# A mixer and mixture-of-experts kernel on one core: the first block's layers written in another order, its input norm done by rows, small loads moved to GpSimd

## What is computed

```python
def first_block(x, ...):
    h = _layernorm(x, ln_in_g, ln_in_b)
    for layer in range(DEPTH):                       # DEPTH = 2
        proj = jnp.einsum('bsd,de->bse', h, w_in[layer])   # 1024 x 4100
        (aq, ak, av, ag, bq, bk, bv, bf, bg, cq, ck, cv, cg) = jnp.split(proj, SPLIT_POINTS, axis=-1)
        # a: rotary, 4 heads, softmax(s1) - lam * softmax(s2), a norm per head
        # b: 4 heads, softmax with a running sum of log_sigmoid(bf) (forgetting)
        # c: 4 heads, stick breaking: exp(log_sigmoid(z) + later log_fail)
        y = concat([oa * silu(ag), ob * silu(bg), oc * silu(cg)]) @ w_out[layer]
        h = _layernorm(DEEPNORM_ALPHA * h + y, ln_g[layer], ln_b[layer])
    return h
```

## Time and profile before

| | us |
|---|---|
| median of 3 runs | 1777.88 (1777.81 to 1778.83) |
| the profiled execution, its own time | 1779.8 |
| its span, first to last instruction | 1777.7 |
| TensorE busy | 1608.0 |
| VectorE, ScalarE busy | 393.0, 299.6 |
| mean granted clock of TensorE | 0.967 of full |

### The profile page before, as it was taken

How to read it: one execution, slowest core, us unless ns; L and a number is a source line. 1 busy time by engine, 2 the same in 40 slices (tenths; PEclk the granted TensorE clock), 3 DMA queues, 4 the chain that set the end, 5 groups by cost and what they waited for, 6 DMA issues and landing times.

```text
span 1777.7 us, 19486 instructions
## 1 busy us (share of the span) xinstructions
PE 1608.0 (90%) x7938; PEld 945.4 (53%) x7938; DVE 393.0 (22%) x881; ACT 299.6 (17%) x586; POOL 2.8 (0%) x9
## 2 busy tenths in 40 slices
PE   3998789997799999998999999999899989998995
PEld 2786577875688777875333434343334333433332
DVE  2012511044233448122110111111111111111111
ACT  2114310143322234102101101010101010101011
POOL 0000000000000000000000000000000000000000
PEclk8999899998899999997999999999999999999998
DMA  7347723354323242335999999999999999999994
GB/s 266 106 145 188 272 95 140 137 212 175 132 95 125 72 142 95 142 136 182 408 428 428 429 428 429 428 429 429 428 429 429 427 429 429 427 429 428 428 428 184
DMA packets 86185, 515.04 MB, mean 290 GB/s; under 512 B 7001, under 2 KB 10777, under 8 KB 61561
## 3 DMA queue, kind: packets, MB, share of 16 engines
q1 hardware_dynamic: 82328, 513.43, 71.8%
q10 hardware_dynamic: 3632, 0.54, 0.2%
q0 software_dynamic: 176, 0.39, 0.1%
HBM read 511.20 MB, written 3.15 MB: 289 GB/s over the span
## 4 chain that ended last, share of the span: by engine, by line
PE 70%; DMA 18%; DVE 6%; ACT 3%; issue 1%; ACTq 1%; SPq 0%; DVEq 0%
PE psum L439 25%; PE psum L979 19%; DMA ring<-in_w_gu 16%; PE psum L1048 9%; PE psum L952 4%; PE psum L448 3%; PE psum L962 2%; DMA ring<-in_w_ada 2%; PE psum L970 1%; DMA w_router<-in_w_router 1%; PE psum L479 1%; PE psum L496 1%; ACT hiddenT L1435 1%; ACT hg L1424 0%; PE psum L473 0%
## 5 line engine op out<-in xcount | busy, mean ns | idle before, releaser
L979 PE MATMUL psum<-ring,hg 128*64 128x512 f32 x2048 | 458.9, 596 | 22.3 <-DMA ring<-in_w_gu 22.3
L439 PE MATMUL psum<-hT,ring 128*128 128x256 f32 x1504 | 337.1, 386 | 6.4 <-ACT hT L1239 6.2
L439 PEld LDWEIGHTS psum<-hT,ring 128*128 128x128 f32 x1504 | 290.4, 194 | 52.0 <-issue 11.7
L979 PEld LDWEIGHTS psum<-ring,hg 128*64 128x64 f32 x2048 | 138.9, 137 | 313.8 <-issue 266.6
L1048 PE MATMUL psum<-w_down,hiddenT 128*64 128x512 f32 x1024 | 229.2, 600 | 28.2 <-ACT hiddenT L1435 25.2
L1048 PEld LDWEIGHTS psum<-w_down,hiddenT 128*64 128x64 f32 x1024 | 74.9, 138 | 162.1 <-issue 162.1
L1849 DVE TENSOR_SCALAR gu<-psum 128x512 f32<-128x512 f32 x32 | 22.1, 692 | 530.4 <-PE psum L979 530.4
L1431 ACT ACTIVATE hidden<-gu 128x512 f32<-128x512 f32 x32 | 20.2, 630 | 317.4 <-DVE gu L1849 317.4
L439 PE MATMUL psum<-yT,ring 128*128 128x256 f32 x256 | 60.7, 403 | 9.3 <-DVE yT L1467 9.3
L952 PE MATMUL psum<-pick,h_tok 128*128 128x128 f32 x512 | 63.4, 284 | 2.9 <-DVE passes L1832 2.9
L952 PEld LDWEIGHTS psum<-pick,h_tok 128*128 128x128 f32 x512 | 60.3, 197 | 8.2 <-issue 8.2
(11 more groups left out here) (346 smaller groups left out, 1203.0 us busy)
## 6 DMA issues: line engine op xcount, KB each, us to landing
ring<-in_w_gu SPq DMA_DIRECT2D x128, 2048.0 KB, 23.4
w_down<-in_w_dn SPq DMA_DIRECT2D x64, 2048.0 KB, 21.1
ring<-in_w_in SPq DMA_DIRECT2D x24, 2048.0 KB, 7.9
...
```

The costliest lines, as they stand in the source:

```text
L439: mm = pe.matmul(bank[0:m, c * T:(c + 1) * T], w[:, k, c0 + c * P:c0 + c * P + m], src[:, k, :], start=(k == 0), stop=(k == k_n - 1))
L979: mm = pe.matmul(psum[half * CAP:(half + 1) * CAP, 4 + part, :], hg[:, k, side, :], w[:, c0:c0 + 512], start=False, stop=(k == KC - 1), sk ...
```

## The change

- **Start.** SP loads the identity alone, then x in two halves, then q and k, and the rest of the constants only behind the second group. VectorE takes mean and variance of each row of x in place (`bn_stats`, `bn_aggr`), ACT the inverse root, VectorE scales x in place, and only then is x turned; gain and shift are applied as the turned x is read. The two norm sums of the input norm on TensorE are gone.
- **Small loads.** ACT issues the two rows of `ln_in`; the other 31 go to GpSimd. What TensorE makes of them (`late_constants`) stands behind q and k of layer 0.
- **Layer.** Scores, running sums and head values stand between the projections; the gates ga come last. Three ada groups are one by one between them, two stand in the norm sums and one behind them. The list of groups follows this order. ACT reads ga, gb, gc unactivated and applies Silu later in one piece; `y_ready` is counted in four parts, and `w_out` takes k in the order 4 to 7, 0 to 3.

The diff, cut to its core:

```diff
-    FIRST_GROUPS = [("q", 0, 512), ("k", 512, 1024), ("va", 1024, 1536), ("ga", 1536, 2048),
-                    ("bqk", 2048, 2560), ("bvfg", 2560, 3076), ("cqk", 3076, 3588), ("cvg", 3588, 4100)]
...
+    FIRST_GROUPS = [("q", 0, 512), ("k", 512, 1024), ("cqk", 3076, 3588), ("bqk", 2048, 2560),
+                    ("bvfg", 2560, 3076), ("", 0, 1), ("va", 1024, 1536), ("", 0, 1), ("cvg", 3588, 4100),
+                    ("", 0, 1), ("ga", 1536, 2048)]
...
-        ada_groups(12 // DEPTH)
+            if name:
+                group(f"{name}{l}", a["w_in"][l], a0, a1)
+            else:
+                ada_groups(1)
         for j in range(2):
             group(f"out{l}.{j}", a["w_out"][l], 512 * j, 512 * j + 512)
+        ada_groups(3)
...
+            ks = range(k_n) if y_ready is None else (4, 5, 6, 7, 0, 1, 2, 3)
...
+                for i, k in enumerate(ks):
+                    if ready == 0 and c == 0 and i % 2 == 0:
+                        read_out(pe, f"x{i}")
+                    elif ready is not None and c == 0 and i % 2 == 0:
+                        pe.wait_ge(ev("h_ready"), 4 * ready + i // 2 - 3)
+                    if y_ready is not None and c == 0 and i % 2 == 0:
+                        pe.wait_ge(ev("y_ready"), 4 * y_ready + i // 2 + 1)
...
+            if aside:
+                ada(aside)
...
-        pe.wait_ge(ev("const_in"), 32)
...
-        norm_sums("in.", [f"x{c}" for c in (0, 2, 4, 6)])
...
-        pe.wait_ge(ev("bcast_in"), 16 * N_BCAST)
-        mm = pe.matmul(bank[0:AH, :], rel_bias[:, :], K["hot"][0:32, :], start=True, stop=True)
...
+        pe.wait_ge(ev("ident_in"), 16)
+        pe.wait_ge(ev("ln_in"), 32)
...
+        for b in range(NB):
+            for c in range(KC):
+                if c % 4 == 0:
+                    pe.wait_ge(ev("x_norm"), 2 * b + c // 4 + 1)
+                at = (c % 2 * NB + b) * P
+                mm = pe.transpose(x_banks[c // 2][:, at:at + P], x_in[:, b, c * P:(c + 1) * P], ident[:, :])
...
+        def late_constants():
...
+            pe.wait_ge(ev("bcast_in"), 16 * N_BCAST)
+            mm = pe.matmul(bank[0:AH, :], rel_bias[:, :], K["hot"][0:32, :], start=True, stop=True)
...
+            if l == 0:
+                late_constants()
...
-            w = weights(f"ga{l}")
+            w = weights(f"cqk{l}")
             for j in range(2):
-                features(f"{L}ga{j}", w, hT, 256 * j, 2)
-            last_of(f"ga{l}", f"{L}ga1")
+                rotate(2 * j)
+                rotate(2 * j + 1)
+                features(f"{L}cqk{j}", w, hT, 256 * j, 2)
+            last_of(f"cqk{l}", f"{L}cqk1")
+            pe.wait_ge(ev("rope"), 4 * l + 4)
             w = weights(f"bqk{l}")
             for j in range(2):
+                for h in (2 * j, 2 * j + 1):
+                    for m in range(2):
+                        head_rows(f"{L}s{h}{m}", qk, h, qk, 4 + h, m)
                 features(f"{L}bqk{j}", w, hT, 256 * j, 2)
             last_of(f"bqk{l}", f"{L}bqk1")
-            w = weights(f"bvfg{l}")
...
-            w = weights(f"cqk{l}")
...
-            pe.wait_ge(ev("rope"), 4 * l + 4)
-            for h in range(HA):
-                for m in range(2):
-                    head_rows(f"{L}s{h}{m}", qk, h, qk, 4 + h, m)
...
-            ada(3)
+            w = weights(f"bvfg{l}")
+            for b in range(NB):
+                tokens(f"{L}bv{b}", w, hT, b, 0, 256 + HB)
+            features(f"{L}gb", w, hT, 256 + HB, 2)
+            last_of(f"bvfg{l}", f"{L}gb")
+            ada(1)
+            w = weights(f"va{l}")
+            tokens(f"{L}va0", w, hT, 0, 0, 512)
...
-            for h in range(HB):
-                head_rows(f"{L}f{h}", bc_qk, h // 2, bc_qk, 2 + h // 2, h % 2)
+            tokens(f"{L}va1", w, hT, 1, 0, 512)
+            last_of(f"va{l}", f"{L}va1")
...
-            ada(3)
-            def turn_a(h):
...
+            ada(1)
+            w = weights(f"cvg{l}")
+            tokens(f"{L}cv0", w, hT, 0, 0, 256)
+            for h in range(HB):
+                head_rows(f"{L}f{h}", bc_qk, h // 2, bc_qk, 2 + h // 2, h % 2)
+            turn_head(l, "a", 0)
+            turn_head(l, "a", 1)
+            tokens(f"{L}cv1", w, hT, 1, 0, 256)
+            read_out(pe, f"{L}va1")
+            head_value(l, "a", 0)
+            head_value(l, "a", 1)
+            turn_head(l, "a", 2)
+            turn_head(l, "a", 3)
+            features(f"{L}gc", w, hT, 256, 2)
+            last_of(f"cvg{l}", f"{L}gc")
+            head_value(l, "a", 2)
+            head_value(l, "a", 3)
+            turn_head(l, "f", 0)
+            turn_head(l, "f", 1)
+            ada(1)
+            w = weights(f"ga{l}")
+            features(f"{L}ga0", w, hT, 0, 2)
+            head_value(l, "f", 0)
+            head_value(l, "f", 1)
+            turn_head(l, "f", 2)
+            turn_head(l, "f", 3)
...
-            pe.wait_ge(ev("y_ready"), l + 1)
+            head_value(l, "f", 2)
+            head_value(l, "f", 3)
+            features(f"{L}ga1", w, hT, 256, 2)
+            last_of(f"ga{l}", f"{L}ga1")
...
+            norm_sums(L, [f"{L}out{j}" for j in range(4)], aside=2)
+            ada(1)
...
-        sp.dma_start(x_in[:, :, :], a["x"][0].rearrange("(b p) d -> p b d", p=P)).then_inc(ev("x_in"), 16)
-        for pack in (False, True):
-            sp.dma_start(const_tiles[pack][:, :], packs[pack][1][:, :]).then_inc(ev("const_in"), 16)
...
+        sp.dma_start(const_tiles[False][:, 0:P], packs[False][1][:, 0:P]).then_inc(ev("ident_in"), 16)
+        for b in range(NB):
+            sp.dma_start(x_in[:, b, :], a["x"][0, b * P:(b + 1) * P, :]).then_inc(ev(f"x_in{b}"), 16)
...
+            if g == 1:
+                sp.dma_start(const_tiles[False][:, P:], packs[False][1][:, P:]).then_inc(ev("const_in"), 16)
+                sp.dma_start(const_tiles[True][:, :], packs[True][1][:, :]).then_inc(ev("const_in"), 16)
...
+        for tile, at, n, src in row_loads[2:]:
+            pool.dma_start(vec_rows[at:at + n, tile, :], src).then_inc(ev("rows_in"), 16)
...
+        for dst, src in alike:
+            pool.dma_start(dst, src.partition_broadcast(P)).then_inc(ev("bcast_in"), 16)
...
+        pool.dma_start(w_router[:, :, :], a["w_router_2"][0].rearrange("(k p) n -> p k n", p=P))\
+            .then_inc(ev("bcast_in"), 16)
+        pool.wait_ge(ev("h_ready"), 4 * (DEPTH + 2))
...
-        for tile, at, n, src in row_loads:
-            act.dma_start(vec_rows[at:at + n, tile, :], src).then_inc(ev("rows_in"), 16)
...
+        for tile, at, n, src in row_loads[:2]:
...
-        norm("in.", True, lambda c: vec("ln_in_g", c), lambda c: vec("ln_in_b", c), hT, 0)
...
+        for b in range(NB):
+            act.wait_ge(ev("x_stats"), b + 1)
+            f(x_rstd[:, b:b + 1], x_mean[:, b, 1:2], ACT.Ln, bias=eps[:, 0:1])
+            f(x_rstd[:, b:b + 1], x_rstd[:, b:b + 1], ACT.Exp, ev("x_rstd"), scale=-0.5)
...
+            x, at = product(act, f"x{c // 2 * 2}"), c % 2 * T
+            ins = act.activation(hT[:, c, :], x[:, at:at + T], ACT.Identity, bias=vec("ln_in_b", c),
...
+            if l == 0:
+                read_out(act, "vecs")
...
-                read(f"{L}ga{j}", gate[:, 2 * j:2 * j + 2, :], ACT.Silu)
+                read(f"{L}cqk{j}", bc_qk[:, 4 + 2 * j:6 + 2 * j, :])
...
+            for h in range(HC):
+                read(f"{L}z{h}", zs[:, h, :], cols=slice(0, W3), scale=HEAD ** -0.5)
+            act.wait_ge(ev("a_max"), l + 1)
+            row_exp(act, sc, 0, 8, row_max, row_sum, 0, 8, ev("a_exp"))
...
-            read(f"{L}gb", gate[:, 4:6, :], ACT.Silu)
...
+            read(f"{L}gb", gate[:, 4:6, :])
+            f(ls[:, :, :], zs[:, :, :], ACT.Abs)
+            f(ls[:, :, :], ls[:, :, :], ACT.Exp, scale=-1.0)
+            f(ls[:, :, :], ls[:, :, :], ACT.Ln, ev("c_ln"), bias=1.0)
...
+            for b in range(NB):
+                read(f"{L}va{b}", va[:, b, :])
+            read(f"{L}cv0", vbc[:, 0, 256:512], cols=slice(0, 256))
+            act.wait_ge(ev("c_exponent"), l + 1)
+            f(zs[:, :, :], zs[:, :, :], ACT.Exp, ev("wc"))
+            turned("a", 0)
+            turned("a", 1)
...
+            f(gate[:, 4:8, :], gate[:, 4:8, :], ACT.Silu, ev("gbc_silu"))
+            f(gate[:, 0:2, :], gate[:, 0:2, :], ACT.Silu, ev("ga_silu"))
+            read(f"{L}ga1", gate[:, 2:4, :], ACT.Silu)
...
+        for b in range(NB):
+            dve.wait_ge(ev(f"x_in{b}"), 16)
+            for j in range(2):
+                ch.after(dve.bn_stats(x_stats[:, b, j, :], x_in[:, b, 512 * j:512 * j + 512]))
+            ch.after(dve.bn_aggr(x_mean[:, b, :], x_stats[:, b, :, :]), ev("x_stats"))
...
+                ts(x_in[:, b, r], x_in[:, b, r], x_mean[:, b, 0:1], x_rstd[:, b:b + 1], ALU.subtract, ALU.mult,
...
+            ins = dve.tensor_scalar(hT[:, c, :], x[:, at:at + T], vec("ln_in_g", c), vec("ln_in_b", c),
...
+            dve.wait_ge(ev("a_exp"), l + 1)
...
+            weigh_a(0)
+            read_out(dve, f"{L}bv1")
```

(14 more changed lines are left out.)

262 lines of the change are left out of this document (128 added, 134 removed).

## The result

| | before | after |
|---|---|---|
| median, us | 1778.36 (1777.81 to 1779.81, 4 runs) | 1701.93 (1699.42 to 1703.73, 4 runs) |
| profiled execution, span | 1779.8, 1777.7 | 1703.73, 1701.9 |
| TensorE busy, granted clock | 1608.0, 0.967 | 1580.8, 0.980 |
| second block begins (profile) | 487.65 | 412.45 |

The account below looks back on a forecast made before the run. It took the first block to be bound by load order at the start and TensorE's waits, with half clock behind them, in the layers. Terms summed to -64.7 us: 1779.8 to 1715.1, less 1.9, forecast 1713, range 1702 to 1731.

Parts of the forecast that it names:

- q begins: Start: first q product at 15.0 us instead of 42.45, once its weights land; -27.4 us, between -29.5 and -24.5.
- q and k, two layers: First projections of a layer: they keep their 29.82 us, half-clock start included; no change.
- late constants: Behind q and k of layer 0: bias row and vectors moved there, +1.4 us if all small loads land by 44.8.
- bodies, with leftovers: End of k up to `w_out`: all waits and three ada groups go, -22.5 and -17.8 us, with +3 left over.
- `w_out`, twice: Output projection of both layers: follows a busy engine, so runs at full clock; -5.4 us.
- norms, twice: Between `w_out` and what follows: two ada groups (3.6 us) replace a 1.6 us wait; +2.0 each layer, +4.0 us.
- some 3 us a layer: Layer bodies: half-clock time inside busy times given back, counted only in the range's lower end.
- the leftovers' +3: Both layer bodies: waits remaining at `logf` (margin nil) and yT's last quarter; +3 us, between 0 and +8.
- Small loads late: Rival, behind q and k: TensorE waits at the bias row, then half clock; 1720 or 1729 us, chance 0.17.
- Hand-overs as the bound: Rival, layers: ScalarE–VectorE hand-overs stay the bound, half of 29.5 idle us return; 1725 us, chance 0.17.
- Slower than before: Rival, first block: GpSimd issues cost over 3.2 us each, gain gone; 1804 us at 4 us, chance 0.03.
- A start set by x: Rival, start: x rather than weights sets q; at most 5 us less gain, inside the range, no separate chance.

Follow-up runs that it names:

- The gap kernels: One or three extra VectorE passes ahead of logf in layer 1, against the changed kernel with its bias write in eight pieces (1696.72 us): 1696.74 and 1701.40 us.
- `start_only`: The new start with the layers of before, against the kernel before: 1749.54 us, ratio 0.9832.
- `layers_only`: The start of before with both layers in the new order, against the kernel before: 1726.11 us, ratio 0.9705.

## Why the prediction was wrong

By its own terms (profiled executions; before is the earlier trace rows, or 11.85, 29.56 and 26.88 us for the stages between):

| term | predicted | measured |
|---|---|---|
| q begins | -27.4 | -28.9 |
| q and k, two layers | 0 | -1.15 - 1.40 = -2.55 |
| late constants | +1.4 | +1.28 |
| bodies, with leftovers | -22.5 - 17.8 + 3 = -37.3 | -20.78 - 22.22 = -43.0 |
| `w_out`, twice | -5.4 | -2.45 - 2.64 = -5.1 |
| norms, twice | +4.0 | +1.91 + 1.15 = +3.1 |
| sum | -64.7 | -75.2 |

**The step that failed** is the size of the bodies: "If every wait went, the body would be its busy time", less the ada groups, with "The 1.2 GHz part inside these busy times I leave in". That gave 124.3 and 121.8 us. TensorE was busy there for 119.98 and 117.17, 4.3 + 4.6 = 9.0 us less, and q and k, of which I had written "half-clock start included", took 2.55 less. These 11.5 us are more than the whole miss of 10.5. The busy time of a stage is no constant of its work, for two reasons.

The first is the clock. These rows hold all of the half-clock time in the bodies that TensorE was busy in, three of before and one of after (length, TensorE busy, ..., PEclk):

```profile
176.00:183.00 7.00, 7.00 (x28) 4.52 (x21) 0.57 (x3) 1.80 (x9) 0.00 (x0) 0.51 1.04 378
200.00:203.50 3.50, 3.00 (x12) 2.80 (x13) 3.21 (x9) 0.57 (x3) 0.00 (x0) 0.51 1.05 387
409.21:415.00 5.79, 5.00 (x18) 4.24 (x19) 5.26 (x16) 1.47 (x3) 0.00 (x0) 0.50 1.05 388
```
```profile
102.00:108.00 6.00, 6.00 (x8) 2.60 (x9) 4.12 (x10) 0.00 (x0) 0.00 (x0) 0.53 1.03 379
```

Busy time times the missing half is 3.4 + 1.5 = 4.9 us in layer 0 before and 2.5 in layer 1, after it 2.8 and none. So the clock gave back 2.1 + 2.5 = 4.6 us of the 9.0, within the "some 3 us a layer" that the lower end of my range allowed. q and k lost 2.0 and 1.7 us in this way before and none after; 1.1 us of these 3.7 they took longer for reasons that stay open. The gap kernels show how a wait brings such time: 1.7 us behind one of 2 us, 2.8 behind one of 5.6.

The second is the order itself, and it isn't in the prediction at all: some 4.4 us of the 9.0 went at full clock. The two halves of the change show it in layer 1: with the old order (`start_only`) TensorE is busy for 127.39 us in the body, 119.5 without its 2.6 us at half clock and 5.4 of ada groups; with the new one (`layers_only`) for 117.17, at clock 1.00. The plainest place is z of layer 1, the same 16 records (the rows count a neighbour or two with them), in before behind the scores of a, in after between two projections:

```profile
381.34:383.87 2.53, 2.53 (x18) 2.19 (x16) 2.39 (x5) 1.41 (x3) 0.00 (x0) 1.00 1.05 399
```
```profile
273.83:275.44 1.61, 1.61 (x17) 1.46 (x16) 0.00 (x0) 1.10 (x3) 0.00 (x0) 1.00 0.32 28
```

Likewise the turns of b's weights and the values of b and c take 6.08 us of busy time in before (417.10 to 423.69) and 4.67 in after. Short stops between small products, for a bank that is still being read, would count as busy here and would go when projections stand between them; no run tests that.

**The step that was right by accident** is the leftovers' +3. I named `logf` and the last quarter of yT. logf had 0.23 us, a margin as thin as worked out, yT nothing. In their place came 6.03 us for va's ring load and 2.9 us of half clock behind it (9.94 against 7.03 for the same products). I had written of the ada groups: "between two there are at least 13 us of projections, and a group of four back was released long before". Both hold, and neither speaks of the bias write, which the same paragraph ought to have followed through SP's queue: it stood in before's trace too, issued at 117.5 us, in this window:

```profile
144.00:156.00 12.00, 12.00 (x57) 10.58 (x56) 0.00 (x0) 1.36 (x3) 0.00 (x0) 1.00 0.45 49
```

Without it the second block begins at 402.8 us and the miss would have been 20 us, not 10.5: the number came as near as it did by luck.

**The start** was right in its mechanism and 1.5 us too dear: I took only the packs' 5.0 us off q's landing and left the 9.0 us of q's own load in full, while it came 6.3 us earlier (13.5 for 19.8); k's rate, which gave 13, was nearer.

**The rivals.** Small loads late: no, w_router had 6.7 us in hand, and GpSimd issued at 0.50 to 0.55 us for a plain row and 0.94 for w_router, VectorE being busy for 7.69 of the first 13.55 us. The port rule of the Trainium skill, SBUF — State Buffer, "Who interferes with whom", would have shown as issues held up there. Beside the four scalings (9.12 to 11.41 us) they took 0.58 and 0.61 us, 0.1 more at most; whether these scalings ran in a 2-port mode no run here shows, so the rule is neither borne out nor refuted. Hand-overs as the bound: no, 0.23 us of logf at most. Slower than before: no. A start set by x: x and weights came together, so that it would have cost nothing to speak of either way. The case that came was in none of them: all good outcomes at once, plus the clock and the shorter busy time. The chance of 0.96 for faster was sound.
